# The first expert pair's columns made on chip by TensorE, with the slot tables and gate sums behind the first products

## The reference

```python
h = rmsnorm(x, norm_ffn[layer])
glog = xt @ wg_group + bg_group            # 4 groups: the best one is taken
elog = xt @ wg_exp + bg_exp                # 8 experts of that group: the best two
gate = pe / sum(pe) * pg
# every expert: its tokens, gathered
yb = (silu(xb @ w1[e]) * (xb @ w3[e])) @ w2[e]     # w1, w3: 1024x512, w2: 512x1024
y[token] += gate * yb
x = x + y
```

## Time and profile before

| | |
|---|---|
| median of 3 runs | 1523.58 us (1522.99 to 1528.08) |
| the profiled execution, its own time | 1524.23 us |
| its span, first to last instruction | 1522.4 us |
| PE busy, share of the span | 83% |
| DVE, ACT, POOL busy | 24%, 16%, 5% |
| mean over the span of what DMA moved | 324 GB/s |
| mean granted TensorE clock | 0.941 of full |

### The profile page before, as it was taken

One profiled execution on the slowest core, in us unless ns is written; L12 is line 12 of the kernel. 1 busy time (PEld: TensorE's weight loads), 2 busy tenths in 40 slices (PEclk: granted clock), 3 DMA queues, 4 the chain that ended last, 5 costly groups with the idle time before them and its releaser, 6 DMA issues.

```text
span 1522.4 us, 14447 instructions
## 1 busy us (share of the span) xinstructions
PE 1264.8 (83%) x5792; PEld 617.7 (41%) x5792; DVE 358.6 (24%) x807; ACT 249.3 (16%) x442; POOL 81.1 (5%) x94
## 2 busy tenths in 40 slices
PE   6989899999878787787888689978878777887885
PEld 3679776644533232222322236743223222232221
DVE  2064487421431001000100007341000100010006
ACT  3243553332200000000000003310000000000002
POOL 1000000000001000000000000000000000000000
PEclk9999999999969999999999999769989999999998
DMA  9344656426269999999999999129999999999994
GB/s 349 87 101 140 211 154 211 114 77 249 110 234 429 427 427 427 428 427 427 426 424 427 428 413 372 70 102 423 428 427 428 428 427 428 427 426 424 427 415 167
DMA packets 74782, 493.46 MB, mean 324 GB/s; under 512 B 16827, under 2 KB 22619, under 8 KB 49645
## 3 DMA queue, kind: packets, MB, share of 16 engines
q1 hardware_dynamic: 57152, 449.35, 71.9%
q0 software_dynamic: 12928, 34.18, 6.9%
q10 hardware_dynamic: 4661, 9.38, 1.8%
HBM read 480.80 MB, written 36.56 MB: 340 GB/s over the span
## 4 chain that ended last, share of the span: by engine, by line
PE 47%; DMA 44%; DVE 4%; issue 2%; ACT 2%; ACTq 0%; SPq 0%; DVEq 0%; POOLq 0%
DMA ring<-in_moe_w 41%; PE ps L2125 19%; PE ps L1799 5%; PE ps L1806 5%; PE ps L2058 3%; PE ps L2135 3%; PE ps L2115 1%; DMA ring<-in_w_in 1%; PE ps L1848 1%; PE ps L2163 1%; PE ps L2096 1%; PE ps L2310 1%; DMA hn_rows<-arena 1%; PE ps L1829 1%; DVE arena L1292 1%
## 5 line engine op out<-in xcount | busy, mean ns | idle before, releaser
L2125 PE MATMUL ps<-ring,arena 128*64 128x512 f32 x2048 | 494.4, 640 | 149.2 <-DMA ring<-in_moe_w 146.5
L2125 PEld LDWEIGHTS ps<-ring,arena 128*64 128x64 f32 x2048 | 152.1, 147 | 487.5 <-issue 291.1
L2135 PE MATMUL ps<-ring,arena 128*64 128x512 f32 x1024 | 229.9, 601 | 26.7 <-issue 16.6
L1673 DVE TENSOR_TENSOR arena<-arena,ps 128x512 f32<-128x512 f32 x32 | 22.0, 688 | 815.4 <-ACT arena L1128 815.4
L2135 PEld LDWEIGHTS ps<-ring,arena 128*64 128x64 f32 x1024 | 85.4, 138 | 149.2 <-issue 139.2
L1799 PE MATMUL ps<-arena,ring 128*128 128x260 f32 x512 | 119.2, 392 | 0.9 <-ACT arena L852 0.9
L1128 ACT ACTIVATE arena<-ps 128x512 f32<-128x512 f32 x32 | 19.1, 597 | 571.6 <-PE ps L2125 571.6
L1799 PEld LDWEIGHTS ps<-arena,ring 128*128 128x128 f32 x512 | 98.5, 196 | 18.1 <-issue 1.7
L1134 ACT ACTIVATE arena<-ps,arena 128x1024 f32<-128x1024 f32 x32 | 35.6, 1114 | 313.3 <-PE ps L2135 313.3
L1806 PE MATMUL ps<-ring,arena 128*128 128x512 f32 x192 | 86.1, 594 | 0.9 <-DMA ring<-in_w_in 0.9
L769 POOL DMA_INDIRECT arena<-hn_rows,arena x32 | 32.3, 1011 | 561.9 <-PE ps L2268 544.6
(11 more groups left out here) (288 smaller groups left out, 942.6 us busy)
## 6 DMA issues: line engine op xcount, KB each, us to landing
ring<-in_moe_w SPq DMA_DIRECT2D x96, 4096.0 KB, 22.8
ring<-in_w_in SPq DMA_DIRECT2D x7, 2048.0 KB, 20.3
y_rows<-c_zero POOLq DMA_DIRECT2D x2, 4160.0 KB, 18.1
ring<-y_rows SPq DMA_DIRECT2D x8, 1024.0 KB, 14.2
arena<-in_x_prompt SPq DMA_DIRECT2D x8, 512.0 KB, 5.8
ring<-in_w_out SPq DMA_DIRECT2D x2, 2048.0 KB, 12.6
hn_rows<-arena POOLq DMA_DIRECT2D x8, 512.0 KB, 3.3
arena<-i_rows SPq DMA_DIRECT2D x8, 256.0 KB, 7.3
```

Of the source, the lines that this page charges most:

```text
L2125: last = T.matmul(ps[r_, 2 + j, :], xgT[:, k, r_], w1v[:, slot, k, :], start=(k == 0), stop=(k == KC - 1))
L2135: last = T.matmul(ps[r_, 5 + c, :], hactT[:, k, r_], w2v[:, piece_slot(half, 2), k, c * 512:(c + 1) * 512], start=(k == 0), stop=(k == FC ...
```

## The change

1. PE makes the columns of pair 0 itself. DVE's new `first_members` writes `first`, a 0/1 matrix of tokens by 128 slots, straight from the first two columns of the rank (experts 0 and 1), and PE's new `rows_of_first` multiplies the tile's rows in SBUF (`hall`) with it, 8 products of 128 columns for each of the five tiles, added up in two PSUM banks. POOL's gather and PE's eight transposes for pair 0 go.
2. `columns` of pair 0 comes before the slot tables, gates and the table of full experts on DVE. `gate_sums` moves on PE between the products with w1 and those with w3 of pair 0.
3. The later tiles' `members` (p = 2 to 4) and `slot_sums` come after the `first` matrices and after `rows_of_first`. In layer 0 the fifth tile's `turn_h` goes ahead of a `slot_sums` and a `ranks`. The rank of p = 3 gets a PSUM bank of its own.
4. ACT's exponential of the gates comes, in layer 0, ahead of its issue of eight loads of pooling constants (L1117 to L1122).

```diff
+        first = [at(lo, TILES, 2, CAP) for lo in (26900, 3072)]
 ...
-                gather(l, xg, xslot[:, 0:1], xg_in)
                 pool.wait_ge(x_turned, PAIRS * l + 1)
                 gather(l, xg, xslot[:, 1:2], xg_in)
 ...
+                act.wait_ge(mem_ready, TILES * (l + 1))
+                nc.scalar.activation(dexp, dexp, ACT.Exp).then_inc(gexp_ready, 1)
                 if l == 0:
 ...
+                def first_members(p):
+                    t = TILE_ORDER[l][p]
+                    dve.wait_ge(rank_done, TILES * l + p + 1)
+                    rank = ps[:, RANK_BANK[p], t * NE:t * NE + 2]
+                    link(V.scalar_tensor_tensor(rank_below[:, t, :], mem[:, t, 0:2], -BELOW, rank, ALU.mult, ALU.add))
+                    V.tensor_tensor(first[l][:, t], wide(iota_below, [P, 2, CAP], 1), wide(rank_below[:, t, :], [P, 2, CAP], 2),
+                                    ALU.is_equal).then_inc(member_ready, 1)
 ...
+                first_members(TILES - 1)
+                for p in range(2, TILES):
+                    members(p)
+                columns(0, True)
                 dve.wait_ge(slots_summed, l + 1)
 ...
+                def rows_of_first(p):
+                    t = TILE_ORDER[l][p]
+                    n = rows_of(t)
 ...
+                    pe.wait_ge(hn_ready, TILES * l + p + 1)
+                    pe.wait_ge(member_ready, 2 * TILES * l + FIRST_AT[p])
+                    for k in range(KC):
+                        last = T.matmul(ps[:, ROWS_BANK[l] + k // 4, (k % 4) * P:(k % 4 + 1) * P], hall[0:n, t, k:D:KC],
+                                        first[l][0:n, t].rearrange("p a c -> p (a c)"), start=(p == 0 and k % 4 == 0),
+                                        stop=(p == TILES - 1), skip_group_check=True)
+                    if p == TILES - 1:
+                        last.then_inc(x_turned, 1)
 ...
                 else:
 ...
+                    rows_of_first(0)
+                    turn_h(TILES - 1)
+                    router_logits(TILES - 1)
+                    slot_sums(TILES - 4)
+                    ranks(TILES - 3)
+                    ranks(TILES - 2)
+                rows_of_first(1)
+                rows_of_first(2)
+                ranks(TILES - 1)
+                rows_of_first(3)
+                rows_of_first(4)
+                for p in range(2, TILES):
+                    slot_sums(p)
 ...
                         products(j, (piece_slot(0, j), piece_slot(1, j))).then_inc((w1_used, h_done)[j], 1)
+                        if first and j == 0:
+                            gate_sums()
 ...
-                turn(0, True)
                 pair(0, True, False)
```

More of the change, by code:

```diff
@@ L1587, in members, with columns @@
                                     ALU.is_equal).then_inc(member_ready, 1)
+                def columns(i, at_first):
+                    dve.wait_ge(x_turned, PAIRS * l + i + 1)
+                    if not at_first:
+                        dve.wait_ge(h_done, PAIRS * l + i)
+                    b = ROWS_BANK[l] if at_first else 0
+                    V.tensor_tensor(xgT, ps[:, b:b + 2, :].rearrange("p a (k c) -> p (a k) c", k=4),
+                                    wide(gain_of_rows[:, l, :], [P, KC, 2 * CAP], 2), ALU.mult).then_inc(xT_ready, 1)
                 if l == 0:
@@ L1602, in experts @@
                             route(u - 2)
-                        if u >= 3:
+                        if u == TILES:
+                            roots_of_rows(u - 1)
+                            first_members(u - 3)
+                            first_members(u - 2)
+                        if u in (3, 4):
+                            first_members(u - 3)
                             members(u - 3)
@@ L1629, in experts @@
                         if u in (TILES - 1, TILES):
+                            first_members(u - 4)
                             members(u - 4)
@@ L1678, in gated @@
                     V.tensor_copy(hactT.rearrange("p k c -> p (k c)"), ps[:, 4, :]).then_inc(hactT_ready, 1)
[L1680 to L1688, removed]
                 dve.wait_ge(hn_stored[l], 16 * TILES)
@@ L2217, in experts @@
                     late = TILE_ORDER[0].index(NT)
-                    for u in range(TILES + 2):
-                        if 2 <= u < TILES:
+                    for u in range(1, TILES):
+                        if u >= 2:
                             project_out(u, 0)
@@ L2236, in experts @@
                             ranks(u - 2)
-                else:
[L2238 to L2242, removed]
-                            turn_h(u - 1)
-                        if u >= TILES:
-                            if u == TILES:
-                                router_logits(u - 1)
-                            if u == TILES + 2:
-                                ranks(u - 3)
-                            slot_sums(u - 4)
-                            if u < TILES + 2:
-                                ranks(u - 3)
-                        else:
-                            if u >= 4:
-                                slot_sums(u - 4)
-                            if u >= 3:
-                                ranks(u - 3)
-                            if u >= 1:
-                                router_logits(u - 1)
@@ L2259, in experts @@
-                slot_sums(TILES - 1)
-                gate_sums()
-                def turn(i, first):
-                    pe.wait_ge(xg_in, 16 * PAIRS * l + 16 * i + 16)
-                    if not first:
-                        pe.wait_ge(xT_ready, PAIRS * l + i)
+                    router_logits(TILES - 1)
+                    ranks(TILES - 2)
+                    rows_of_first(0)
+                else:
+                    for u in range(TILES):
+                        mix(u)
+                        maps(u)
+                        if u >= 1:
+                            turn_h(u - 1)
+                        if u >= 4:
+                            slot_sums(u - 4)
+                        if u >= 3:
+                            ranks(u - 3)
+                        if u >= 1:
+                            router_logits(u - 1)
+                    rows_of_first(0)
+                    turn_h(TILES - 1)
+                    router_logits(TILES - 1)
+                    slot_sums(TILES - 4)
+                    ranks(TILES - 3)
+                    ranks(TILES - 2)
```

52 lines of the change are left out of this document (31 added, 21 removed).

## The result

| | before | after |
|---|---|---|
| median, runs taken side by side (20 of each) | 1528.15 us (1522.99 to 1531.48) | 1536.76 us (1527.64 to 1542.34) |
| ratio after to before, 95% interval | | 1.0054 [1.0042, 1.0066] |
| profiled execution, span | 1524.23, 1522.4 us | 1536.76, 1535.0 us |
| mean granted clock | 0.941 | 0.934 |

The change makes the kernel slower by 0.54%, some 8 us, where 11 us faster was forecast. The new mechanism is in place: no gather stands before the first products, and 80 passes of the new product stand in each layer. At full clock a pass of it takes nearly twice what was forecast.

The account below looks back on a forecast made before the run. Expert stages were taken as bound by DMA bytes at 427 GB/s from when pair 0's products free w1; 9.1 (layer 0) + 2.8 (layer 1) - 1.0 = 10.9 us off 1524.2 gives 1513.3, said as 1513, range 1507 to 1521.

Parts of the forecast that it names:

- the price of a pass: In rows_of_first, one pass of 128 by 128 columns: 0.13 us at full clock, 0.22 at half clock.
- A pass of 0.2 us or more at 2.4 GHz: Listed sign, for the new product's passes on PE, that the forecast would be wrong.
- the last rank: Layer 0, PE between the rows of three tiles and of two: six passes, 0.65 us at full clock.
- The gain up to w1's release: Layer 0: w1 of pair 0 is free at 436.8 instead of 445.9, a gain of 9.1 us.
- the three blocks: Layer 1, PE's rows: first tile 3.2 us, two tiles 6.0 while the clock returns, last two tiles 4.2.
- rival A: Clock stays at 1.2 GHz until the first products: layer 0 gains 0.2, layer 1 loses 3.2 to 4.5; 1528 us, chance 0.07.
- the slot sums: Layer 0, on PE before the first products: 24 passes, 1.3 us, hidden inside the wait for columns.
- Cost 0 and 1.0: Loss in us in layers 0 and 1 from gate sums delaying w3's release and the loads behind it.
- still queues behind w1's: Pair 0: w3 is released 9.2 us after w1, whose load takes 9.8, so DMA does not pause.
- 21.9 us of work for DMA: After w1's release DMA is busy this long; w2's load is asked for at 21.1 in layer 0, 22.8 in layer 1.
- the last route of layer 1: DVE's route would start at 999.3 and end at 1003.0, before PE needs it at 1004.7; PE waiting meant wrong.
- The 8-row tile: In rows_of_first, the tile with 8 rows costs as much as the others; priced by rows, 1.8 us better per layer.

Follow-up runs that it names:

- e2: The changed kernel with blocks of 24 float32 products at various strides behind its last work, one execution for the profile: 0.112 us a pass at stride 1, 0.238 at 8.
- e3: The kernel before, with only the gate sums moved between pair 0's products and the columns ahead of DVE's wait; gather kept: 1533.22 us, ratio 1.0038.
- e1: The changed kernel with rows_of_first reading its weights side by side, which leaves pair 0's features in the wrong order: 1517.79 us, ratio 0.9937.
- e4: The changed kernel with ACT writing the rows with features already in order, so all later reads are contiguous: 1513.19, 1515.18 and 1520.46 us, ratios 0.9903, 0.9933, 0.9937.
- e7: The changed kernel with other blocks behind its last work (more strides, both operands strided, 512 moving columns, bfloat16): 0.173 us a pass at stride 3, 0.218 at 16.
- e5: e4 with the gate sums behind both products of pair 0: 1515.84 us, ratio 0.9926, and again 1515.53 us, ratio 0.9922.
- e6: e5 with the first tile's rows of layer 1 behind the ranks of p = 2 and 3: 1517.94 us, ratio 0.9941.
- e8: The changed kernel, strided read kept, with the gate sums behind both products of pair 0: 1528.39 us, ratio 0.9998.

## Why the prediction was wrong

**The step that failed** is the price of a pass: "A pass with 128 stationary and 128 moving columns takes 1.98 / 16 = 0.124 us at full clock; I take 0.13, since these operands are read with a stride of eight." The stride was seen and priced at 0.006 us. It costs 0.12 to 0.13: 0.24 in place of 0.13 (after), 0.238 for 0.112 in e2. At half clock 0.22 was nearly right, for another reason. The earlier trace rows are of a product whose weights lie side by side. It was the nearest row in size, but none of those read from before was of a strided float32 product of few columns; the strided reads of `turn` are transposes, and those cost nothing more. The range took no bound of "twice as long" from anywhere, though the shape wasn't in the trace. "A pass of 0.2 us or more at 2.4 GHz" was named as the first sign of a wrong forecast, and it is what the trace shows.

**By layers.** Layer 0: rows 11.8 + 7.7 where 8.1 + 4.2 was forecast, 7.2 too much, and the products start 28.4 us behind the output projection where 21.2 was forecast: the same 7.2. Two smaller errors cancel: the rows begin 6.2 us behind the projection for 6.9, and the last rank takes 1.4 for 0.65. The gain up to w1's release is 1.9 instead of 9.1. Layer 1: 97.8 us from the last results to the products where 89.2 was forecast; 6.2 of the 8.6 are the three blocks (3.98, 7.67, 7.99 for 3.2, 6.0, 4.2), and 2.0 lie ahead of them.

**The clock, rival A.** It came back sooner than forecast: at 1.2 GHz at 417.0 to 420.0 us and at 2.4 GHz at 421.0, where 4.6 us were taken. But it did not stay: at 428 to 434 and from 1021 to 1028 us it was at 1.2 GHz again, through the first half of the last two tiles' rows in layer 0. The prediction wanted 1.00 there, and said that no stretch showed a falling clock for full 128-column work; after does. It cost these passes nothing, since they take 0.24 us at either clock. So rival A, which priced them at 0.22 because of the clock, gave the right sign by luck and about half the size: 4 us slower, where 8.6 were measured. What it described happened in part, and it isn't what the loss is made of. The first products of layer 0 ran at 2.4 GHz, 7.09 us for 32, as forecast, where e3, whose PE had waited for the gather, took 10.02. In layer 1 they took 8.25: the slot sums, put at nothing inside the wait for `columns`, stand ahead of them in the chain and the clock was at 1.2 GHz from 1022 to 1027 us.

**The gate sums.** "Cost 0 and 1.0" was too small. The length of 2.1 us was right. Two things were missed. The first is that the results behind the sums can run at a lower clock: they take 8.57 us in e3, 8.78 in e1 and in e4 and 9.61 in e7, for 7.09 with the sums behind (e5, e6, e8). In both profiles of after itself they take 7.09, so there this costs nothing. The second is the argument that w3's load "still queues behind w1's", which looked at that transfer only. The binding one is w2's, which waits for the results; the dip stands there, not between w1 and w3. The prediction had this wait in its sum, 21.9 us of work for DMA against 21.1 and 22.8, and trusted a margin of 0.8 us. In after the results end 20.5 us behind w1's release (446.33 to 466.80), and DMA dips all the same. Behind the release layer 0 then takes 2.4 to 5.6 us more than before (478.2 and 481.4 for 475.8), and nothing was put down for this. e3, which has the gate sums alone, takes 3.2 more (479.0). PE did not wait ahead of the sums, and not for the last route of layer 1 either: it began late, at 1008.25 us where 999.3 was forecast, but the last rank's passes follow the rows of two tiles without a break at 1015.5.

**What held.** The 8-row tile costs as much as the others: on the average of both layers a pass of 8 rows lasts 0.431 us, as the page counts it with its overlap, and one of 128 rows 0.422. From the first pair's results to the last the stage of layer 0 takes 457.2 us before and 457.7 in the second profile of after, but 460.9 in the first, in which the last results also ran slower (8.57 for 7.10); the rest of that difference is not explained. With a contiguous read the products of layer 0 start 19.2 us behind the output projection, 2.0 better than forecast, and the kernel comes to 1513 to 1520 us where 1513 was forecast. That is luck in part: its rows take 13.0 and 15 to 16 us to the products where 14.3 and 19.9 were forecast, and its first pairs lose more than forecast. The path of the forecast was right; what failed in it is the size of one term. The forecast and the median lie 19.5 us apart as the runs beside each other count it (-10.9 against +8.6). The blocks of the new product account for 7.2 + 6.2 = 13.4 of it. The rest is the time ahead of them, the first products of layer 1 and the gate sums.

**What stays open.** Where the rest of e3's delay of 3.5 us goes, beyond the 1.4 of the dip; why the clock falls during the rows; why e4 falls into two groups; and why a strided float32 operand is slow.

## What to carry to other kernels

Read the access pattern of each operand before taking a duration from a row of the same shape: here a float32 product of 128 moving columns took twice the time with its stationary operand at a stride of 4, 8 or 16 elements or its moving one at 8, and a transpose of the same data did not warn of it. Turn the data once where an engine with time to spare writes it, and look up what the turned write costs there (here 0.9 us a tile on ACT). When work is put between a release and the next, follow the chain to the transfer that is asked for last, here w2's, and look at the granted clock behind thin passes.

## What the runs showed that was not expected

- The stride's price has steps: 0.112 us a pass at 1, 0.118 at 2, 0.173 at 3, 0.233 at 4, 0.238 at 8, 0.218 at 16; both operands at 8 (e7) take (1592.61 - 1581.01) / 48 = 0.242, no more than one.
- It doesn't depend on TensorE's clock: 13 passes in 3 us at 0.50, 14 at 1.00.
- Unchanged work ahead of the change takes different times in different profiles, sometimes of one kernel: the last two pooling products of layer 1 (x16 in the chain) take 4.71 and 4.94 us in before, 5.96 and 5.98 in both profiles of after, 4.74 and 4.95 in e8. In e2 and e7, whose work up to there is that of after, the last three take 4.7, 5.7 to 5.8 and 5.8, and 3.55, 5.96 and 5.98 in after. The three profiles of e4 show both: 5.93 and 5.95 in the execution of 1519.95 us, 3.55 and 5.2 to 5.3 in those of 1510.02 and 1509.72. Single profiles of one kernel so lie 10 us apart, and a difference of a few microseconds is read only from medians or from the length of one named block.
